# Attention of a two-layer block: values multiplied into the keys once per block of keys, instead of once per head and query block

## What is computed

```python
q = (cq @ w_uq).reshape(B, L, N_HEADS, KV_LORA)          # 8 heads x 128
kv = rmsnorm(c_kv, kv_norm_g)                            # 1024 x 128
# an indexer picks 256 keys per query, as a mask here
logits = q . kv * KV_LORA ** -0.5 + bias
probs = softmax(where(selected and causal, logits, -inf))
o = einsum("bthk,btkc->bthc", probs, kv)                 # 128 channels a head
o = einsum("bshc,hcd->bshd", o, w_uv)                    # down to 64 a head
y_attn = o.reshape(B, L, 512) * silu(g_attn)
```

## Time and profile before

| | us |
|---|---|
| median of 3 runs | 3045.54 (3043.31 to 3049.46) |
| profiled execution, first to last instruction | 3044.6 |
| TensorE, VectorE, ScalarE, GpSimd busy | 2860.1, 1953.3, 1323.3, 1280.0 |
| attention stage of layer 0, first logits to last turn_y | 486.1 to 683.5 |

### The profile page before, as it was taken

The page is one execution under the profiler, slowest core; times in us unless marked ns, Lnnn a source line. Parts: engine busy times, 40 slices in busy tenths (PEclk is TensorE's granted clock), DMA queues, the critical chain, the costliest instruction groups (busy, mean ns, idle before and its releaser), DMA issues.

```text
span 3044.6 us, 49166 instructions
## 1 busy us (share of the span) xinstructions
PE 2860.1 (94%) x19746; PEld 1749.1 (57%) x19746; DVE 1953.3 (64%) x3140; ACT 1323.3 (43%) x2341; POOL 1280.0 (42%) x1060
## 2 busy tenths in 40 slices
PE   7889998999979988999999999999999999999998
PEld 3438776874429667864466565664764444444443
DVE  3785997763589996644875665666663654444445
ACT  3353654652366646643344554454543322122222
POOL 1302482010602580012545846767661635555551
PEclk9999999999989999999999999999999999999999
DMA  8223241002201340021101111201122201111111
GB/s 292 110 70 122 84 154 52 12 22 104 94 14 43 125 139 29 12 87 59 67 29 42 70 42 42 70 31 66 43 85 110 70 28 56 56 56 44 54 44 74
DMA packets 50898, 213.45 MB, mean 70 GB/s; under 512 B 4680, under 2 KB 9968, under 8 KB 34032
## 3 DMA queue, kind: packets, MB, share of 16 engines
q1 hardware_dynamic: 42288, 195.63, 18.5%
q10 hardware_dynamic: 8384, 14.68, 1.4%
HBM read 190.36 MB, written 19.94 MB: 69 GB/s over the span
## 4 chain that ended last, share of the span: by engine, by line
PE 41%; DVE 3%; POOL 3%; ACT 2%; issue 1%; DMA 0%; ACTq 0%; POOLq 0%; DVEq 0%
PE big L284 7%; PE big L286 7%; PE big L285 7%; PE banks L284 4%; PE banks L286 4%; PE banks L285 4%; PE banks L1183 3%; POOL w_lo L596 2%; PE banks L1162 0%; PE banks L1153 0%; PE banks L1134 0%; PE banks L1164 0%; PE banks L1170 0%; DVE arena L2567 0%; DVE arena L2568 0%
## 5 line engine op out<-in xcount | busy, mean ns | idle before, releaser
L653 POOL TENSOR_TENSOR w_lo<-stage,w_hi 128x512 bf16<-128x512 f32 x340 | 429.7, 1295 | 367.3 <-ACT w_hi L1390 367.0
L646 POOL CAST w_hi<-stage 128x512 bf16<-128x512 f32 x252 | 179.6, 753 | 781.4 <-PE big L286 588.5
L284 PE MATMUL big<-w_hi,ht_hi 128*128 128x256 bf16 (+2 forms) x1280 | 358.0, 288 | 22.7 <-DVE arena L1913 4.7
L596 POOL TENSOR_TENSOR w_lo<-stage,w_hi 128x512 bf16<-128x512 f32 x174 | 249.6, 1445 | 263.6 <-ACT w_hi L1590 263.6
L285 PE MATMUL big<-w_lo,ht_hi 128*128 128x256 bf16 (+2 forms) x1280 | 357.9, 288 | 0.0
L286 PE MATMUL big<-w_hi,ht_lo 128*128 128x256 bf16 (+2 forms) x1280 | 357.8, 287 | 0.0
L284 PE MATMUL big<-ht_hi,w_hi 128*128 128x512 bf16 x816 | 310.2, 380 | 24.7 <-POOL w_lo L596 8.7
L286 PE MATMUL big<-ht_hi,w_lo 128*128 128x512 bf16 x816 | 310.0, 380 | 0.0
L285 PE MATMUL big<-ht_lo,w_hi 128*128 128x512 bf16 x816 | 309.8, 380 | 0.0
L284 PE MATMUL big<-arena,w_hi 128*128 128x512 bf16 (+1 forms) x716 | 222.5, 328 | 21.4 <-DVE arena L2154 8.4
L285 PE MATMUL big<-arena,w_hi 128*128 128x512 bf16 (+1 forms) x716 | 222.6, 328 | 0.0
(11 more groups left out here) (395 smaller groups left out, 7144.2 us busy)
## 6 DMA issues: line engine op xcount, KB each, us to landing
stage<-in_w SPq DMA_DIRECT2D x130, 1024.0 KB, 4.8
arena<-in_w_ada SPq DMA_DIRECT2D x48, 512.0 KB, 4.4
arena<-in_x SPq DMA_DIRECT2D x16, 512.0 KB, 9.2
xs<-arena SPq DMA_DIRECT2D x16, 512.0 KB, 2.6
arena<-xs SPq DMA_DIRECT2D x16, 512.0 KB, 7.2
gt<-arena ACTq DMA_DIRECT2D x16, 256.0 KB, 2.5
arena<-gt ACTq DMA_DIRECT2D x16, 256.0 KB, 2.6
out_x<-arena SPq DMA_DIRECT2D x8, 512.0 KB, 2.6
```

Source lines behind the costliest of these rows:

```text
L284: pe.matmul(out, ah, bh, start=start, stop=False, skip_group_check=onto)
L596: return pool.tensor_tensor(lo, x, hi, ALU.subtract)
L646: pool.tensor_copy(w_flat[0][:, w0 + c0:w0 + c1], stage[:, n % RAW_RING, c0:c1]).then_inc(s_w_hi_split, mark(s_w_hi_split, n, q))
L653: ins = pool.tensor_tensor(w_flat[1][:, w0 + c0:w0 + c1], stage[:, n % RAW_RING, c0:c1], w_flat[0][:, w0 + c0:w0 + c1], ALU.subtract)
```

## The change

The product with w_uv is moved ahead of the weighing. `values(s)` multiplies block s of keys with all of w_uv once (128 x 512, three matmuls of 512 columns, into a big tile), at head 5 of block s - 1, and for s = 0 ahead of the first logits. High and low part go to VAL. `weigh` now has PT stationary and the head's 64 columns of VAL moving, and writes 64 columns of one tile that holds the whole block (pool "ov", one bank). Line 2360's division reads that tile straight from PSUM, at head 4 instead of 5. KVK, OT and the copies into YR go. The pool of turned probabilities has three banks, PB three buffers; `turn` is two steps behind `logits`, `weigh` four, `turn_y` at head 6. The loads of x wait for the last `weigh`, and the chunk uv is done with at block 6, head 5.

```diff
-        pools = {"big": two[0:2], "q": [(big[i // 2][:, i % 2 * 512:i % 2 * 512 + 512], (i,)) for i in (2, 3, 0, 1)], "t": one[0:2], "o": one[2:4], "c": one[0:3], "f": one[3:4], "c2": two[2:4], "mlp": two, "u": one[0:1], "p2": one[1:2], "p5": one[2:3]}
+        pools = {"big": two[0:2], "q": [(big[i // 2][:, i % 2 * 512:i % 2 * 512 + 512], (i,)) for i in (2, 3, 0, 1)], "t": one[0:2], "o": one[2:4], "c": one[0:3], "pt": one[0:3], "ov": one[3:4], "f": one[3:4], "c2": two[2:4], "mlp": two, "u": one[0:1], "p2": one[1:2], "p5": one[2:3]}
...
-        KVK = [bf(at + 3072, 1024).rearrange("p (s c) -> p s c", s=NT), bf(at + 3584, 1024).rearrange("p (s c) -> p s c", s=NT)]
+        VAL = [bf(4096 + 2048 * i, 4096).rearrange("p (s c) -> p s c", s=NT) for i in range(2)]
...
-        PB = [fl(at, 1024), fl(at + 1024, 1024)]
+        PB = [fl(at, 1024), fl(at + 1024, 1024), fl(11392, 1024)]
...
-        OT = [[bf(at, 128), bf(at + 64, 128)], [bf(at + 128, 128), bf(at + 192, 128)]]
...
-                        sp.wait_ge(s_weigh, when(s_weigh, "uv", l, NT - 1, NH - 1))
+                        sp.wait_ge(s_weigh, when(s_weigh, "ov", l, NT - 1, NH - 1))
...
-                pe.wait_ge(s_latent_dve, when(s_latent_dve, "kv_n", l))
-                g = take(pe, "big", "kvtok", l)
-                for s in range(NT):
-                    ins = pe.transpose(g[:, s * P:(s + 1) * P], RAW[:, s * P:(s + 1) * P], ident)
-                ins.then_inc(s_gemm, mark(s_gemm, "kvtok", l))
...
-                        g = take(pe, "t", "pt", l, tb, h, q0)
+                        g = take(pe, "pt", "pt", l, tb, h, q0)
...
-                def weigh(tb, h, g):
-
+                def values(s):
+
+                    g = take(pe, "big", "v", l, s)[:, 0:512]
+                    mm3(pe, g, [x[:, s * P:(s + 1) * P] for x in KVT], [x[:, 0, 0:512] for x in uv], True, True).then_inc(s_turn, mark(s_turn, "v", l, s))
+
+                def weigh(tb, h):
+
+                    if h == 0:
+                        pe.wait_ge(s_v_lo, when(s_v_lo, l, tb))
+                        take(pe, "ov", "o", l, tb)
                     pe.wait_ge(s_pt_lo, when(s_pt_lo, l, tb, h))
+                    g = tile("ov", "o", l, tb)[:, h * 64:(h + 1) * 64]
                     for s in range(tb + 1):
-                        ins = mm3(pe, g[:, 0:P], [x[:, s, :] for x in KVK], [x[:, s * P:(s + 1) * P] for x in PT[h % 2]],
-                                  s == 0, s == tb)
+                        ins = mm3(pe, g, [x[:, s * P:(s + 1) * P] for x in PT[h % 2]], [x[:, s, h * 64:(h + 1) * 64] for x in VAL], s == 0, s == tb)
                     ins.then_inc(s_weigh, mark(s_weigh, "ov", l, tb, h))
-
-                def values(tb, h, g):
-
-                    pe.wait_ge(s_ot_lo, when(s_ot_lo, l, tb, h))
-                    ins = mm3(pe, g[:, P:P + 64], OT[h % 2], [x[:, 0, h * 64:h * 64 + 64] for x in uv], True, True)
-                    ins.then_inc(s_weigh, mark(s_weigh, "uv", l, tb, h))
...
                 n = len(steps)
                 queries(0)
-                for i in range(n + 8):
-                    if 8 <= i and steps[i - 8][1] == NH - 1:
-                        turn_y(steps[i - 8][0])
+                values(0)
+                for i in range(n + 7):
+                    if 7 <= i and steps[i - 7][1] == NH - 1:
+                        turn_y(steps[i - 7][0])
                     if i < n:
                         logits(*steps[i])
                         if steps[i][1] == 3 and steps[i][0] < NT - 1:
                             queries(steps[i][0] + 1)
                             if steps[i][0] == NT - 2:
                                 chunk_used(l, "uq", s_gemm)
-                    if 3 <= i < n + 5:
-                        g = take(pe, "o", "o", l, i)
-                    if 3 <= i < n + 3:
-                        weigh(*steps[i - 3], g)
-                    if 5 <= i < n + 5:
-                        values(*steps[i - 5], g)
-                    if 1 <= i <= n:
-                        turn(*steps[i - 1])
-                chunk_used(l, "uv", s_weigh)
+                    if 4 <= i < n + 4:
+                        weigh(*steps[i - 4])
+                    if 2 <= i < n + 2:
+                        turn(*steps[i - 2])
+                    if i < n and steps[i][1] == 5 and steps[i][0] < NT - 1:
+                        values(steps[i][0] + 1)
+                        if steps[i][0] == NT - 2:
+                            chunk_used(l, "uv", s_turn)
...
-                act.wait_ge(s_gemm, when(s_gemm, "kvtok", l))
-                act.activation(KVK[0], tile("big", "kvtok", l)[:, :].rearrange("p (s c) -> p s c", s=NT), ACT.Copy).then_inc(s_latent_act, mark(s_latent_act, "kvtok_hi", l))
...
+                def values_high(s):
+                    act.wait_ge(s_turn, when(s_turn, "v", l, s))
+                    act.activation(VAL[0][:, s, :], tile("big", "v", l, s)[:, 0:512], ACT.Copy).then_inc(s_v_hi, mark(s_v_hi, l, s))
+
                 queries(0)
...
+                values_high(0)
+                for i in range(n + 7):
+                    if 7 <= i and steps[i - 7][1] == NH - 1:
+                        tb = steps[i - 7][0]
...
-                    if 2 <= i < n + 2:
-                        tb, h = steps[i - 2]
+                    if 3 <= i < n + 3:
+                        tb, h = steps[i - 3]
                         for q0 in range(0, tb + 1, 4):
                             m = min(tb + 1, q0 + 4) - q0
                             act.wait_ge(s_turn, when(s_turn, "pt", l, tb, h, q0))
-                            if i >= 4:
-                                act.wait_ge(s_weigh, when(s_weigh, "ov", l, *steps[i - 4]))
-                            act.activation(PT[h % 2][0][:, q0 * P:(q0 + m) * P], tile("t", "pt", l, tb, h, q0)[:, 0:m * P], ACT.Copy).then_inc(s_pt_hi, mark(s_pt_hi, l, tb, h, q0))
-                    if 6 <= i < n + 6:
-                        tb, h = steps[i - 6]
-                        act.wait_ge(s_weigh, when(s_weigh, "uv", l, tb, h))
-                        if h == 0 and tb >= 2:
-                            act.wait_ge(s_gemm, when(s_gemm, "yt", l, tb - 2))
-                        act.activation(YR[tb % 2][:, h * 64:h * 64 + 64], tile("o", "o", l, i - 1)[:, P:P + 64], ACT.Copy).then_inc(s_yr, mark(s_yr, l, tb, h))
-                        freed(s_yr, "o", l, i - 1)
-                    if 4 <= i < n + 4:
-                        tb, h = steps[i - 4]
-                        act.wait_ge(s_weigh, when(s_weigh, "ov", l, tb, h))
-                        if i >= 6:
-                            act.wait_ge(s_weigh, when(s_weigh, "uv", l, *steps[i - 6]))
-                        act.activation(OT[h % 2][0], tile("o", "o", l, i - 1)[:, 0:P], ACT.Copy).then_inc(s_ot_hi, mark(s_ot_hi, l, tb, h))
+                            if i >= 5:
+                                act.wait_ge(s_weigh, when(s_weigh, "ov", l, *steps[i - 5]))
+                            act.activation(PT[h % 2][0][:, q0 * P:(q0 + m) * P], tile("pt", "pt", l, tb, h, q0)[:, 0:m * P], ACT.Copy).then_inc(s_pt_hi, mark(s_pt_hi, l, tb, h, q0))
+                    if 1 <= i <= n and steps[i - 1][1] == 5 and steps[i - 1][0] < NT - 1:
+                        values_high(steps[i - 1][0] + 1)
                     if i < n:
                         tb, h = steps[i]
                         N = (tb + 1) * P
                         act.wait_ge(s_lmax, when(s_lmax, l, tb, h))
...
+                        act.activation(PB[i % 3][:, 0:N], PB[i % 3][:, 0:N], ACT.Exp, scale=-1.0, bias=s_(S_NMX + i % 3), accum_out=s_(S_SUM8 + tb % 2 * 8 + h)).then_inc(s_prob, mark(s_prob, l, tb, h))
                         if h == 3 and tb < NT - 1:
                             queries(tb + 1)
...
-                dve.wait_ge(s_latent_act, when(s_latent_act, "kvtok_hi", l))
-                dve.tensor_tensor(KVK[1], tile("big", "kvtok", l)[:, :].rearrange("p (s c) -> p s c", s=NT), KVK[0], ALU.subtract).then_inc(s_latent_dve, mark(s_latent_dve, "kvtok_lo", l))
-                freed(s_latent_dve, "kvtok", l)
...
+                def values_low(s):
+                    dve.wait_ge(s_v_hi, when(s_v_hi, l, s))
+                    dve.tensor_tensor(VAL[1][:, s, :], tile("big", "v", l, s)[:, 0:512], VAL[0][:, s, :], ALU.subtract).then_inc(s_v_lo, mark(s_v_lo, l, s))
+                    freed(s_v_lo, "v", l, s)
...
+                values_low(0)
...
-                    if 2 <= i < n + 2 and steps[i - 2][0] >= 4:
-                        turned_lo(*steps[i - 2], 0)
+                    if 3 <= i < n + 3 and steps[i - 3][0] >= 4:
+                        turned_lo(*steps[i - 3], 0)
+                    if 1 <= i <= n and steps[i - 1][1] == 5 and steps[i - 1][0] < NT - 1:
+                        values_low(steps[i - 1][0] + 1)
                     if i < n:
                         tb, h = steps[i]
                         N = (tb + 1) * P
```

(30 more changed lines are left out.)

23 lines of the change are left out of this document (9 added, 14 removed).

## The result

The changed kernel takes 3097.77 us (median of 4 runs, 3093.62 to 3101.2), the kernel before 3045.47 beside it: ratio 1.0171, 95% interval 1.0156 to 1.0185. Slower, as forecast, but by 52 us where 16.6 were forecast, and outside the range.

What follows compares the result with a forecast made beforehand. TensorE's work bounds most of the stage, but in block 4 a ScalarE and VectorE ring does. Per layer, stage +8.3, latents -2.0, clock +2; twice that, +16.6 us, gives 3062 us, range 3038 to 3086.

Steps and rivals of the forecast that it cites:

- (a): Head 4: next block's first weighing waits until VectorE empties the output bank; 4.2 us between reductions in block 3, 2.0 before.
- (b): Logits 6 wait for the values' tile until VectorE has subtracted them; 5.6 us to the next reduction in block 4.
- the sum: Layer stage by blocks 1 to 7, reduction to reduction: +2.1, +2.3, +2.3, +0.7, +2.5, +1.6, -1.0 us; block 0 unchanged.
- the clock: TensorE's drop to 1.2 GHz after waits: 2 us a layer taken; bounds nothing to 24 us over both layers.
- The steps untouched by them: Heads 0 to 2 stay 3.1 and 3.4 us apart in blocks 5 and 6; block 7 steps 3.6 to 3.7.
- The 64-column matmul: Weighing: 864 matmuls a layer fall from 0.056 to 0.029 us each, saving 23.3 us of TensorE.
- rival 5: A load sets a matmul's pace, so 64 columns take 0.056 us like 128; 3074 us, chance 0.04.
- Latents: Ahead of the scores, eight transposes, a copy and a 1.23 us subtraction go: 2.0 us off a layer, bounds 0 and 2.7.
- tail: Last reduction to last turn_y of a layer's stage: 11.85 us falls to about 9.05, -2.8 us.
- the ring: From block 4, reduction, Exp, copy of turned probabilities, subtraction, next reduction set the step: 2.91 us in block 4, left unchanged.
- R: Start of the reduction from which the waits are counted; in block 4 the weighing's wait ends 1.98 us behind it.
- rival 4: The clock falls in every block; 3082 to 3086 us, chance 0.08.

Runs made afterwards that it cites:

- experiments 5: Changed kernel with idle matmuls (the fillings) ahead of head 0's weighing, ten, and behind turn_y directly ahead of logits 6, eight: 3065.91 us, ratio 1.0059.
- experiment 1: Changed kernel with VectorE's reciprocal and multiply out of the block's bank one turn earlier, ahead of the queries' subtraction: 3040.26 us, ratio 0.9983.
- experiment 3: Changed kernel with the division moved to head 3 and the values put in a bank of the turned probabilities: 3019.41 us, ratio 0.9915.
- experiment 6: The kernel of experiment 3 with every weighing done twice: 3030.51 us, ratio 0.9957.
- experiment 7: The kernel of experiment 3 with two banks for turned probabilities and the third for the values alone: 3033.14 us, ratio 0.9964.
- experiment 2: Changed kernel with the values' product in a bank of turned probabilities instead of a big tile: 3066.64 us, ratio 1.0060.

## Why the prediction was right and wrong

**The sign and the two waits: right.** Both waits came where they were put: (a) seven times a layer; (b) in six blocks, 2.3 to 2.9 us each in layer 0 (the profile's other two fall into block 0). Without the low clock (table, fourth column) every one of blocks 1 to 7 is within 0.8 us of the forecast, mostly within 0.5, and the whole stage, first to last reduction, is 195.1 and 196.8 us where the sum gave 185.0 + 10.5 and 183.9 + 10.5. In layer 0 some of that closeness is luck: block 0, for which nothing was forecast, is 1.4 us shorter (14.4 for 15.8), and blocks 1 to 7 together are 11.5 us longer, not 10.5. The waits' own price at the full clock follows from experiments 5, 1 and 3. Wait (a) is head 4 with the fillings less head 4 without (a): 1.6, 1.9, 2.3, 1.4, 1.7, 2.0 and 2.4, together 13.3 us a layer. Wait (b) is head 5 in the same way, with experiment 3: 1.2, 1.4, 1.55, 1.1, 1.3 and 1.4, together 7.9. Twice 21.2 is 42 us; with the 32 of the clock that is 74 of the 78 that experiment 3 gave back. The total came out less well than the blocks: with both fillings the kernel is 20.4 us slower than the one before, where the terms other than the clock gave 12.6. The tails hold 2.2 of the difference and the stages 1.9; the rest isn't placed.

**The steps untouched by them: right.** Heads 0 to 2 of block 5 are 3.14 us apart, of block 6 3.38, of block 7 3.62, the queries' step of block 3 4.88. The saving of TensorE reached the end only in part, as experiment 6 shows from the other side. Block 7, without queries and values, is shorter at the full clock (28.4 for 29.1, forecast 28.1), and experiment 7 confirms that it needs the third bank for that.

**The 64-column matmul: right.** A weighing in block 6 after, seven blocks of keys by three matmuls, the first and the last row of 21:

```profile
655.36 0.19 PE L283 MATMUL banks<-arena 128*128 128x64 bf16 x1
...
655.94 0.19 PE L285 MATMUL banks<-arena 128*128 128x64 bf16 x1
```

20 steps in 0.58 us, 0.029 each, each with its own load; rival 5 is out. By this the Trainium skill's figure for pairs of load and matmul (TensorE: Matmul & The Clock Gate, Back-to-back issue gap), 81 ns at 128 columns, does not hold here: 128 columns took 0.056 us.

**Latents and tail.** Ahead of the scores a reciprocal of layer 1 and the long accumulate stood at 838.65 and 863.79 before; after:

```profile
858.00 6.54 DVE L2039 RECIPROCAL arena<-arena 128x1024 f32<-128x1024 f32 x1
...
881.21 2.78 DVE L2073 SCALAR_TENSOR_TENSOR arena<-arena,small 128x384 f32<-128x384 f32 x4
```

The lag falls from 19.35 to 17.42: 1.9 us gained, 2.0 taken. The tail, last reduction to last turn_y, is 10.16 us for 11.85: 1.7 gained where 2.8 were taken. In layer 0 the lead grows only from 1.4 at that reciprocal (127.36 for 128.75) to 2.3 at the first reduction, so about 1.0 of the latents' gain is left there, less than programs that are the same up to there differ between executions.

**The step that failed: the clock.** "I take 2 us a layer, nearer the lower end, as TensorE has room wherever the ring rules." With the clock held up by the fillings the stage is 10.1 us shorter in layer 0 (205.2 - 195.1) and 20 in layer 1 (216.8 - 196.8); that is what the term measured. Even the upper bound, 12 us a layer, was too low for layer 1. Three things were wrong in it. First, the length of the waits: I worked out when a wait ends (1.98 us behind R, and it was 1.96) but took TensorE to arrive just ahead of R. At head 3 VectorE works on the queries, and TensorE is through with its next logits before R (in block 4 it is idle from 573.18, and R is 574.04), so a wait is 3.2 us in the mean, up to 4.1, not 1.7 to 2.9. This leaves the reductions where they are, which is why the sum didn't need it, but it is idle time all the same. Second, the bound of one stretch of 3.4 us in a block: a stretch of 6.8 us began in wait (a) of block 6 in layer 0 (639.1 to 645.9, shown above) and one in that of block 7 in layer 1, and one of 13.6 in that of block 1 in layer 1. Third, the argument for the lower end was upside down. Where the ring rules, TensorE has room as long as it can run ahead; behind a wait it cannot, since ScalarE and VectorE have run dry too and their next work hangs on its turn and its logits, so there every lost tenth is on the path. Its being idle before is what brought the clock down. This is rival 4, which I gave 0.08 and 3082 to 3086 us, and which was itself sized by that same bound. Half of the low-clock time agrees in size: (1 - 0.93) x 2 x 205 = 29 us low in layer 0 and (1 - 0.86) x 2 x 217 = 61 in layer 1, less 4 and 12 with the fillings, halved: 12 and 24 us.

The Trainium skill tells of this pattern (TensorE: Matmul & The Clock Gate, HAM oscillation — how this bites in real kernels): a wait that recurs in every round of a loop lets each round begin at half the clock, and its remedy is an order of the loop that keeps the array fed. The trace agrees in the main: among blocks 1 to 7 the clock fell in six of layer 0 and in all of layer 1, while block 4 of layer 0 stayed at 1.00 with the same two waits (2.82 and 2.70 us), and without the waits both stages stood at 0.98.

Two sums of the forecast are off by a little, without effect on its number: four transposes in 0.47 us are 0.12 each, not 0.11 (about 2 us more of TensorE's work a layer, before and after), and 3062 with 24 us for the clock in place of 4 is 3082, not 3080.

What stays open: why layer 1's stage fell to the lower clock twice as long as layer 0's with the same waits. The sums of the waits are equal, and with the fillings both stages are equal to 1.7 us; no run separates it further. With wait (b) alone (experiment 1) both stages stand at 0.94, with (a) alone (experiment 2) at 0.95 and 0.92.

## What to carry to other kernels

When a change adds a wait, work out both its ends: the end sets the next step, but the idle time before it is set by how far ahead the waiting engine had come, and on TensorE that idle time can be paid a second time through the clock, here 32 of 52 us. When work is moved or a tile is shared, put the release where the releasing engine is idle anyway: two VectorE instructions, one turn earlier and ahead of the queries' subtraction, took back 57 us, some 27 of it the wait itself and the rest the clock around it. And a saving on an engine that isn't the bound of a stage is a licence to reorder (a third bank, then a later turn, then a shorter ring), not a gain by itself: only with the ring opened and the queries put first did this change come to 2% faster.
